# Output projection, norm 1 and embedding gate in one block, with norm 1 applied to the products instead of the operand

## The reference

```
mix = jnp.concatenate([y_ssd, y_gla, y_mla], axis=-1) @ lw["w_out"]
x = _layernorm(DN_ALPHA * x + mix, lw["ln1_g"], lw["ln1_b"])
a, b = jnp.split(x @ lw["ffn_w_up"], 2, axis=-1)
full_f = jnp.concatenate([ffn_buf0, a], axis=1)
a = _causal_dwconv(full_f, lw["ffn_conv_w"], lw["ffn_conv_b"])
f = (jax.nn.gelu(a, approximate=False) * b) @ lw["ffn_w_down"]
ple = jax.nn.sigmoid(x @ lw["ple_w_gate"]) * (pl @ lw["ple_w_proj"])
x = _layernorm(DN_ALPHA * x + f + ple, lw["ln2_g"], lw["ln2_b"])
```

## Time and profile before

| what | value |
|---|---|
| runs | 2656.22, 2667.15 and 2682.72 us, median 2667.15 us |
| span of the profiled execution, from its first to its last instruction | 2667.4 us |
| PE busy | 2310.9 us (87%) |
| DVE, ACT, POOL busy | 916.7, 813.8, 657.1 us |

### The profile page before, as it was taken

How to read it: one execution, slowest core, us unless ns; L and a number is a source line. 1 busy time by engine, 2 the same in 40 slices (tenths; PEclk the granted TensorE clock), 3 DMA queues, 4 the chain that set the end, 5 groups by cost and what they waited for, 6 DMA issues and landing times. The chain is left out here.

```text
span 2667.4 us, 38846 instructions
## 1 busy us (share of the span) xinstructions
PE 2310.9 (87%) x16043; PEld 2092.2 (78%) x16043; DVE 916.7 (34%) x1506; ACT 813.8 (31%) x1471; POOL 657.1 (25%) x332
## 2 busy tenths in 40 slices
PE   4996677899987999989969785688998989999896
PEld 3995363498977999989859763446997889999896
DVE  2415562211123243335425067421111314343453
ACT  4322323222214222233344232323221232222334
POOL 0332040000022234334323223200000323434341
PEclk7997565778788999999989875657797999999998
DMA  3323102022111232222033301201230102222220
GB/s 109 106 40 97 40 5 84 7 73 96 63 36 41 79 96 94 77 84 88 24 109 80 104 5 36 84 6 40 80 119 4 64 31 90 95 94 95 66 80 34
DMA packets 168754, 177.14 MB, mean 66 GB/s; under 512 B 47199, under 2 KB 151303, under 8 KB 166341
## 3 DMA queue, kind: packets, MB, share of 16 engines
q1 hardware_dynamic: 163884, 132.51, 16.3%
q0 software_dynamic: 4608, 41.95, 4.3%
q10 hardware_dynamic: 100, 0.46, 0.1%
HBM read 166.04 MB, written 8.86 MB: 66 GB/s over the span
## 5 line engine op out<-in xcount | busy, mean ns | idle before, releaser
L324 POOL TENSOR_TENSOR w_low<-ring,w_high 128x1024 fp32r<-128x1024 f32 x120 | 291.2, 2427 | 678.2 <-ACT w_high L320 678.2
L343 PE MATMUL ps<-x_high,w_high 128*128 128x272 f32 x1664 | 347.0, 290 | 28.3 <-DVE x_low L334 22.3
L343 PE MATMUL ps<-x_high,w_low 128*128 128x272 f32 x1664 | 346.0, 289 | 0.0
L343 PE MATMUL ps<-x_low,w_high 128*128 128x272 f32 x1664 | 345.7, 289 | 0.0
L320 ACT ACTIVATE w_high<-ring 128x1024 fp32r<-128x1024 f32 x166 | 174.8, 1055 | 544.5 <-PE ps L343 489.2
L343 PEld LDWEIGHTS ps<-x_high,w_high 128*128 128x128 f32 x1664 | 262.8, 190 | 30.0 <-DVE x_low L334 23.2
L343 PEld LDWEIGHTS ps<-x_high,w_low 128*128 128x128 f32 x1664 | 262.4, 189 | 0.0
L343 PEld LDWEIGHTS ps<-x_low,w_high 128*128 128x128 f32 x1664 | 262.3, 189 | 0.0
L343 PE MATMUL ps<-x_high_in,w_high 128*128 128x272 f32 x736 | 154.3, 291 | 45.5 <-POOL w_low_in L324 45.5
L2183 DVE TENSOR_SCALAR arena<-arena,parb 128x560 f32<-128x560 f32 x44 | 84.6, 1922 | 277.3 <-ACT arena L2131 277.3
L1708 PE MATMUL ps<-xc 128*128 128x16 f32 x1024 | 176.6, 308 | 0.6
(11 more groups left out here) (376 smaller groups left out, 3959.8 us busy)
## 6 DMA issues: line engine op xcount, KB each, us to landing
ring<-in_ffn_w_up SPq DMA_DIRECT2D x44, 1024.0 KB, 5.3
ring<-in_ffn_w_down SPq DMA_DIRECT2D x20, 1024.0 KB, 5.1
ring<-in_w_in SPq DMA_DIRECT2D x18, 1024.0 KB, 5.4
ring<-in_w_out SPq DMA_DIRECT2D x8, 1024.0 KB, 9.0
ring<-in_ple_w_gate SPq DMA_DIRECT2D x8, 1024.0 KB, 5.0
big<-in_state_ssm SPq DMA_DIRECT2D x16, 256.0 KB, 5.1
out_ssm_sample<-big SPq DMA_DIRECT2D x4, 1024.0 KB
arena<-in_x_prompt SPq DMA_DIRECT2D x1, 2048.0 KB
```

What stands on the lines that cost most here:

```text
L324: pool.tensor_tensor(low[:, i % 2], ring[:, n % RING, :, c0:c0 + P], wh[:, i % 2].bitcast(F32), ALU.subtract).then_inc(s_low, 1)
L343: last = pe.matmul(ps[:, b + h, 0:HALF], w[:, i % 2, k, :], x[:, k, h * HALF:(h + 1) * HALF], start=(k == 0 and x is x_high and w is wh), ...
```

## The change

Norm 1 is no longer made on `xT` before the gate product. With r the unnormed residual sum, u its mean, s its reciprocal deviation per token, g and b gain and bias per feature, LN(r) @ W equals s * ((r*g) @ W) - (u*s) * (g @ W) + b @ W. So the kernel now multiplies r*g, split into high and low, and appends the two columns g and b to the moving operand of each half: a matmul moves 274 columns instead of 272, and the last two columns of a product tile are g @ W and b @ W. Mean and variance are needed only when a tile is taken out of PSUM.

Part by part:

- The three blocks become one. PE goes from the eighth output tile straight to the first gate tile; behind six of its eight chunks it makes the statistics (4 matmuls with the mean matrix: sum of the chunks, sum of the squares), then the last two chunks.
- During the output projection ACT also makes `x_high` from each residual chunk and its square, POOL adds up the squares (`add_square`), DVE makes `x_low`. All this goes on beside the output tiles.
- `rstd1` and `shift1` (minus mean times reciprocal deviation) are made by ACT and DVE while PE works on the gate. The table of ScalarE functions with Ln and Exp is loaded at the start of the block.
- `unnormed` takes a product tile out of PSUM on DVE: a copy of the two extra columns to `gbias`, a multiplication by `rstd1` (one operand in PSUM), and an addition of `shift1` times g @ W (both tensors in SBUF). The term b @ W is the bias of the next ACT instruction, or is added by the last DVE instruction.
- In the gate part each tile is unnormed before its sigmoid, and DVE and ACT also norm `xT` itself, chunk by chunk, for the later residual.
- In the up part DVE unnorms a tile (into `cv`) before ACT copies it to `ab`, and b tile (into `hT`) before the product with Gelu, which becomes a `scalar_tensor_tensor` with both tensors in SBUF. ACT waits for `s_an`, and so does PE in place of `s_ac` before it reuses a's banks.
- The embedding rows are loaded when the output projection is done.

```diff
+        norm = sb("norm", [P, 2, T])
+        rstd1, shift1 = norm[:, 0], norm[:, 1]
+        gbias = sb("gbias", [P, 2, 2, 2])
...
+        def split_steps(e, i, b, low, x_high, x_low, k0, k1, x_ready=None):
+
+            n = HX if len(x_high.shape) == 4 else HALF
+            for k in range(k0, k1):
                 if x_ready is not None:
-                    e.wait_ge(x_ready, k + 1)
+                    e.wait_ge(x_ready, k + (3 if n == HX else 1))
                 for w, x in ((wh, x_high), (wh, x_low), (low, x_high)):
                     for h in range(2):
-                        last = pe.matmul(ps[:, b + h, 0:HALF], w[:, i % 2, k, :], x[:, k, h * HALF:(h + 1) * HALF],
+                        moving = x[:, k, h] if n == HX else x[:, k, h * HALF:(h + 1) * HALF]
+                        last = pe.matmul(ps[:, b + h, 0:n], w[:, i % 2, k, :], moving,
                                          start=(k == 0 and x is x_high and w is wh),
                                          stop=(k == KD - 1 and w is low))
...
+        def unnormed(bank, dst, gb):
+
+            dve.tensor_copy(gb, ps[:, bank, HALF:HX])
+            dve.tensor_tensor(two(dst), halves(bank), two(rstd1), ALU.mult)
+            dve.drain()
+            return dve.scalar_tensor_tensor(out=dst, in0=shift1, scalar=gb[:, 0:1], in1=dst, op0=ALU.mult, op1=ALU.add)
...
                 @block.scalar
                 def _(e):
+                    act.preload_act_table_set("natural_log_exp_and_others")
                     e.dma_start(rows_b[0:3, :], a["ffn_conv_w"][L]).then_inc(s_ffr, 16)
...
+                    def residual_high(m):
+
+                        e.wait_ge(s_res, m + 1)
+                        act.activation(xh[:, m, :, 0:HALF], two(xT[:, m]), ACT.Copy, scale=col(m, G1)).then_inc(s_xh, 1)
+                        if m >= 2:
+                            e.wait_ge(s_sqs, max(1, m - 2))
+                        act.activation(sqb[:, m % 2], xT[:, m], ACT.Square).then_inc(s_sq, 1)
...
-            layer_norm("ln1", lambda k: col(k, G1), lambda k: col(k, B1), summed=True,
-                       ahead=(split_gate_high, split_gate_low))
...
                     for m in range(KD):
+                        e.wait_ge(s_wl, KD + m + 1)
+                        if m < 2:
+                            e.wait_ge(s_res, KD - 1 + m)
+                        else:
+                            e.wait_ge(s_gt, m - 1)
+                        if m == 0:
+                            split_steps(e, m, 4, wl, xh, xl, 0, KD - 2, s_xl)
+                            statistics()
+                            split_steps(e, m, 4, wl, xh, xl, KD - 2, KD, s_xl).then_inc(prod, 1)
+                        else:
+                            split_product(e, m, 4 + 2 * (m % 2), wl, xh, xl)
...
+                        unnormed(4 + 2 * (m % 2), gt[:, m % 2], gbias[:, m % 2, 0]).then_inc(s_gt, 1)
+                        dve.tensor_tensor(xT[:, m], xT[:, m], rstd1, ALU.mult)
+                        e.drain()
+                        dve.tensor_tensor(xT[:, m], xT[:, m], shift1, ALU.add).then_inc(s_xn, 1)
...
-                            act.activation(ab[:, i, 2:2 + HALF], ps[:, b, 0:HALF], ACT.Copy)
-                            act.activation(ab[:, i, 2 + HALF:2 + SEQ], ps[:, b + 1, 0:SEQ - HALF], ACT.Copy)
+                            e.wait_ge(s_an, m0 + (q + 1))
+                            act.activation(ab[:, i, 2:2 + SEQ], cv[:, i, 0:SEQ], ACT.Identity, bias=gbias[:, i, 0, 1:2])
...
-                            e.drain()
-                            e.wait_ge(s_ac, m0 + (q + 1))
                             if not (first and q < 2):
                                 e.wait_ge(s_gl, m0 + (q - 1))
+                            e.wait_ge(prod, 2 * m0 + (PR_UP + 2 * q + 1))
+                            unnormed(4 * i, cv[:, i, 0:T], gbias[:, i, 0]).then_inc(s_an, 1)
+                            e.wait_ge(s_ac, m0 + (q + 1))
...
+                            e.wait_ge(prod, 2 * m0 + (PR_UP + 2 * q + 2))
+                            hm = hT[:, bass.ds(m, 1), :].rearrange("p o t -> p (o t)")
+                            unnormed(4 * i + 2, hm, gbias[:, i, 1])
+                            e.drain()
                             e.wait_ge(s_gl, m0 + (q + 1))
-                            e.wait_ge(prod, 2 * m0 + (PR_UP + 2 * q + 2))
-                            dve.tensor_tensor(two(hT[:, bass.ds(m, 1), :].rearrange("p o t -> p (o t)")),
-                                              two(ga[:, i, :]), halves(4 * i + 2), ALU.mult).then_inc(s_hd, 1)
+                            dve.scalar_tensor_tensor(out=hm, in0=hm, scalar=gbias[:, i, 1, 1:2], in1=ga[:, i, :],
+                                                     op0=ALU.add, op1=ALU.mult).then_inc(s_hd, 1)
```

More of the change, by code:

```diff
@@ L1914, in _ @@
-                @block.vector
-                def _(e):
-                    low_x(e, ml, mixT, mh, s_mh, s_ml)
-                    for m in range(KD):
-                        e.wait_ge(prod, PR_OUT + m + 1)
-                        dve.scalar_tensor_tensor(out=two(xT[:, m]), in0=two(xT[:, m]), scalar=ALPHA,
-                                                 in1=halves(2 * (m % 4)), op0=ALU.mult, op1=ALU.add
-                                                 ).then_inc(s_res, 1)
-                        add_to_sum(e, m, s_res, s_sum)
-                    e.wait_ge(s_sum, KD - 1)
@@ L1971, in _ @@
+                    low(0)
+                    low(1)
+                    for i in range(2, KD + 1):
+                        low(i)
+                        if i >= 3:
+                            add_square(i - 2)
+                    add_square(KD - 1)
+                    for i in range(KD + 1, 2 * KD):
+                        low(i)
                     for part in range(2):
-                        e.wait_ge(s_wh, KD - 1 + part)
+                        e.wait_ge(s_wh, 2 * KD + 1 + part)
@@ L1994, in _, with statistics @@
                     for m in range(KD):
-                        if m >= 2:
-                            e.wait_ge(s_wl, m - 1)
-                            e.wait_ge(s_sg, m - 1)
-                        split_product(e, m, 4 + 2 * (m % 2), wl, xh, xl, s_xl if m == 0 else None)
+                        e.wait_ge(s_wl, m + 1)
+                        if m >= 4:
+                            e.wait_ge(s_res, m - 3)
+                        split_product(e, m, 2 * (m % 4), wl, mh, ml, s_ml if m == 0 else None)
+                    def statistics():
+                        e.wait_ge(s_sum, KD - 1)
+                        e.wait_ge(s_sqs, KD - 1)
+                        for b, x in ((0, sum1), (2, sqs)):
+                            for h in range(2):
+                                last = pe.matmul(ps[:, b + h, 0:HALF], C("mean"), x[:, h * HALF:(h + 1) * HALF],
+                                                 start=True, stop=True)
+                        last.then_inc(s_st, 1)
+                    for m in range(KD):
+                        e.wait_ge(s_wl, KD + m + 1)
[9 more added lines that the diff above has]
+                            split_product(e, m, 4 + 2 * (m % 2), wl, xh, xl)
                         if m == 1:
@@ L2033, in _ @@
-                    for part in range(2):
-                        weights_in(e, LD_UP + part)
-                        high_weights(part, LD_UP + part, 0, s_wh)
-                    e.wait_ge(s_wh, KD)
-                @block.vector
-                def _(e):
-                    low_x(e, xl, xT, xh, s_xh, s_xl)
+                        if m >= 2:
+                            e.wait_ge(s_sg, m - 1)
+                        unnormed(4 + 2 * (m % 2), gt[:, m % 2], gbias[:, m % 2, 0]).then_inc(s_gt, 1)
```

197 lines of the change are left out of this document (115 added, 82 removed).

## The result

The changed kernel takes 2627.26 us (median of 20 runs, 2605.97 to 2662.44); the kernel before, with its further runs, 2663.89 us (20 runs, 2640.60 to 2683.77). The ratio is 0.988, 95% interval 0.9855 to 0.9904: faster by 1.2%. Three of the 20 runs and four of the 20 before, more than 1.5% above the fastest of their kernel, are in a slower state and left out of the ratio (as in the table of the experiments), and the medians of the others are 2623.61 and 2655.03 us. The forecast was 2626.6 us, 1.5% less than before (0.985). The time was hit to a microsecond, but the gain, 31 to 37 us by these medians, is 4 to 9 us short of the 40.8 forecast, and single runs of one kernel lie up to 56 us apart: that the time agrees so closely is luck.

The account below looks back on a forecast made before the run. PE was taken to bound the up block, a DVE and ACT chain the stretch between output projection and gate. Per layer -25.0 + 2.3 + 0.5 + 1.8 = -20.4; two layers -40.8, 2667.4 to 2626.6 us; range 2612 to 2653.

Parts of the forecast that it names:

- The gap: Between output projection and gate: PE goes on with only the statistics between, 32.85 us become 7.9, gain 25.0 us a layer.
- All four conditions: At the gate's start: summed squares, last low part, second tile's weights and shift are ready in time, squares by 1.0 us.
- Two more columns: Gate and up matmuls: 274 instead of 272 columns cost 0.92 ns each, a loss of 2.3 us a layer, ends 0 and 2.3.
- Embedding: Behind the last gate tile: DVE's unnorming gives PE its first bank back late, loss 0.5 us, ends 0 and 1.4.
- Table load: At the block's start: ACT's table load fits before the first weights, 0 us; up to 1.3 if DMA issues wait.
- the 2628.4 us by that page: Forecast total if the table load also needs a drain, 2.66 us in all, sticking out 1.8 us in both layers.
- The gate's other tiles and the up loop: Extra DVE and ACT work per gate tile and up pair stays covered behind PE: 0 us for each.
- the other order: Up loop, POOL's weight split starting before DVE's addition: b weights at t+11.8, t being when the a tile is done.
- Both are under t+12.0: Up loop: b weights arrive at t+10.6 with DVE first or t+11.8 with POOL first, before PE wants them at t+12.0.
- The first rival: PE waits in the up loop for late b weights, 0.5 us a pair, 22 us in all: 2649 us; chance 0.15.
- The tail: Up block's end: DVE's longer last product costs 1.8 us a layer; ends 1.4, and 4.4 with transposes at the lower clock.
- Third rival: PE still waits between output projection and gate for late squares or last low part, 5 us a layer: 2637; chance 0.10.

Follow-up runs that it names:

- after: The changed kernel itself, against the kernel before: 2627.26 us, ratio 0.988.
- after_again: The changed kernel unaltered, run and profiled a second time: 2624.06 us, ratio 0.9849 to the kernel before.
- e1: The changed kernel with 272 instead of 274 columns in every gate and up matmul, halves still 274 columns apart: 2615.92 us, ratio 0.9847.
- e2: The changed kernel with the operand's halves 276 instead of 274 columns apart, still 274 columns in a matmul: 2610.91 us, ratio 0.9808.
- e3: The changed kernel with 276 columns in every gate and up matmul, halves 276 columns apart: 2624.11 us, ratio 0.9853.
- e5: The changed kernel with PE making the statistics ahead of the first gate tile and waiting for the shift: 2644.93 us, ratio 0.9925.
- e10: The changed kernel with 272 columns in every gate and up matmul, halves 276 columns apart: 2640.65 us (one run).

## Why the prediction was right, and where its sum was off

- **The gap** (-25.0): right, in mechanism and size. The statistics cost 1.63 us on PE, 1.85 was the price taken. All four conditions held. The squares were summed at 815.89, 0.76 us before PE wanted them (forecast 1.0); the shift came at 822.34, 10.1 us behind the last residual (9.8), under the second gate tile. The kernel that waits for the factors shows that this condition was worth 11 of the 24.4 us.
- **Two more columns** (+2.3 a layer, +1.95 of it in the up block): the mis-sized term. By the loops it is 4.7 and 2.9 us, or 22 x 0.173 = 3.8 against the 12.04 of the runs with 272 columns at 1104 bytes. Of the 0.173, 0.08 to 0.12 is columns, about what proportion has (0.09); the rest is the spacing of the halves, which the prediction did not consider. I had set the upper end of this term at the proportional 2.3, and that was too low.
- **Embedding** (+0.5): +0.4 in the first profile, +1.4 and +1.0 in the second, where POOL comes ahead of DVE. The mechanism, PE waiting for a bank that DVE gives back late, holds, but the delay came from meeting POOL, which the prediction left out of this term; its upper end of 1.4 was reached.
- **Table load** (0): right. The load takes 1.28 us, the DMAs are issued beside it and the first weights follow 0.08 us behind it. The Trainium skill ("ScalarE: Activation LUTs", section "What ACT_TABLE_LOAD costs") adds a drain of 1.38 us; here the trace shows none in that place, and the 2628.4 us by that page were not needed.
- **The gate's other tiles and the up loop** (0): right in result, PE has no wait in either. The chain was right to 0.1 us up to the convolution's end (t+6.35, forecast t+6.4); behind it POOL's pass took 2.82 instead of 2.40 us, so the b weights came at t+11.05, not t+10.6. For the other order the forecast t+11.8 was 0.9 short: 0.3 up to the copies, 0.2 in the convolution, 0.5 behind, most of it POOL's 2.81. "Both are under t+12.0" was the step that failed, without showing in the time, since DVE comes first, by 0.35 us in the pair shown and by 0.20 to 0.36 in the others that POOL meets. The first rival was nearer than its 0.15: a chain 0.2 to 0.4 us later ahead of the addition should meet it, and at 22 x 0.39 us a layer it would take half of the gain.
- **The tail** (+1.8): +1.7 in the second layer, +3.2 in the first, where the transposes behind the wait run at the lower level of the clock (4.08 us for 2.57). The prediction had that as the upper end of 4.4. It is no exception: the second profile has it in both layers.
- **Third rival**: no wait in the seam, so it fell.

That the meetings of DVE and POOL cost what the rows say is shown from both sides. The last product at 985.09, 0.05 us behind POOL's start, ends at 988.02, 0.58 after POOL; POOL, when 0.44 and 0.57 us of a DVE instruction are still ahead, takes 2.69 and 2.82 instead of 2.40. That agrees with the Trainium skill ("SBUF — State Buffer", section "Who interferes with whom"), where whichever is second waits, and it is why the order of these two within a third of a microsecond decides.

## What to carry to other kernels

A normalization in front of a matmul chain can be moved behind it, and what it is worth is read from the idle time of PE at the seam; the gain there was forecast to 0.3 us a layer from the rows. What it costs lies where the deferred work goes: there price the slack of the whole chain in each order in which two engines can meet, not only the likelier, and take the longest duration that the rows show for each instruction. And where a change makes moving rows longer, its layout is a variable of its own: try spacing and width apart.

## What the runs showed of the hardware

- Matmuls of 272, 274 and 276 moving columns, with halves 1104 bytes apart, are 125.4, 126.7 and 126.7 ns apart (pair by 96): the first two extra columns cost 1.25 ns, the next two nothing. With halves 1096 bytes apart, 272 and 274 columns take 126.4 and 127.2 ns. Each figure is from one profile, both layers alike. Only these spacings were tried, and `x_low` starts 128 bytes earlier with 1104; which property counts is open.
- After the same wait of 2.60 us the transposes took 4.08 us in one layer and 2.57 in the other. In the seven profiles that have this wait (2.60 or 2.61 us; `after`, `after_again`, e1, e2, e3, e5, e10) they took 2.57 us six times and 3.90 to 4.24 us eight times; what tells the two apart is open.
- A DVE copy of 16 elements per partition within SBUF, 0.17 us alone, took 2.37 us where POOL was splitting weights (1009.95), and ended 0.03 us after it.
